# A two-block transformer on one core: h copied and used tile by tile at three heads, and two weight halves moved on ScalarE

## The reference

```python
# first block, two layers: three attention branches on one projection of x, gated, merged, normed
proj = x @ w_in                       # MoBA q k v gate, MLA latents and gate, differential q k v gate
out  = merge(moba(...), mla(...), diff(...)) @ w_out
r    = ALPHA * x + out
x    = layernorm(r + sigmoid(r @ w_pg) * (p @ w_p))

# second block, two layers
def second_block(x, ...):
    for i in range(2):
        h = rmsnorm(x, norm_mix[i])
        x = x + hybrid_mixer(h, ...)      # h @ w_in, short convolutions, a state-space part, a gated norm
        h = rmsnorm(x, norm_ffn[i])
        x = x + (swiglu(h, ...) if i == 0 else moe_swiglu(h, ...))   # 8 experts, top 2
    return rmsnorm(x, norm_final)
```

## Time and profile before

| | us |
|---|---|
| median of three runs | 2121.65 |
| the three runs | 2123.34, 2121.65, 2121.0 |
| the profiled execution | 2121.3 |
| its span in the profile | 2119.5 |
| TensorE busy | 2096.3 |
| VectorE, ScalarE, GpSimd busy | 1416.4, 1295.4, 651.4 |

### The profile page before, as it was taken

The page is one execution under the profiler, slowest core; times in us unless marked ns, Lnnn a source line. Parts: engine busy times, 40 slices in busy tenths (PEclk is TensorE's granted clock), DMA queues, the critical chain, the costliest instruction groups (busy, mean ns, idle before and its releaser), DMA issues.

```text
span 2119.5 us, 33547 instructions
## 1 busy us (share of the span) xinstructions
PE 2096.3 (99%) x13311; PEld 1867.1 (88%) x13315; DVE 1416.4 (67%) x1437; ACT 1295.4 (61%) x1424; POOL 651.4 (31%) x316
## 2 busy tenths in 40 slices
PE   9999999999999999999999999999999999999998
PEld 8979999988999999999998888888888888888887
DVE  1555223346422774223777999999999999999997
ACT  4556545455544534444545777777777777777776
POOL 5717886726787204988101000000000000000000
PEclk9999999999999999999999999999999999999999
DMA  7434564625455425655447999999999999999995
GB/s 245 138 105 153 179 198 156 183 75 163 160 188 177 129 91 175 189 193 178 141 140 252 387 376 336 370 360 376 352 351 370 351 375 351 359 356 375 367 365 200
DMA packets 307633, 529.06 MB, mean 250 GB/s; under 512 B 11842, under 2 KB 152802, under 8 KB 307520
## 3 DMA queue, kind: packets, MB, share of 16 engines
q1 hardware_dynamic: 306496, 525.92, 70.9%
q0 software_dynamic: 736, 1.00, 0.2%
q10 hardware_dynamic: 288, 0.52, 0.1%
HBM read 525.84 MB, written 1.05 MB: 249 GB/s over the span
## 4 chain that ended last, share of the span: by engine, by line
PE 90%; POOL 3%; DVE 3%; ACT 2%; DMA 1%; issue 1%; SPq 0%; DVEq 0%; POOLq 0%
PE bank L720 88%; POOL weights_low L3092 3%; PE bank L1525 1%; DVE qb L2354 1%; DMA ring<-in_w_in_dram 1%; ACT sc L1670 1%; ACT weights_high L1673 0%; DVE sc L2362 0%; DMA ring<-in_w_ple_dram 0%; DVE h L2362 0%; PE bank L929 0%; PE bank L731 0%; DVE nmax L2389 0%; ACT expert_weights_high L1673 0%; ACT xT L1670 0%
## 5 line engine op out<-in xcount | busy, mean ns | idle before, releaser
L2354 DVE TENSOR_TENSOR expert_weights_low<-ring_experts,expert_weights_high 128x2048 fp32r<-128x2048 f32 x336 | 764.7, 2288 | 72.6 <-ACT expert_weights_high L1673 72.5
L1673 ACT ACTIVATE expert_weights_high<-ring_experts 128x2048 fp32r<-128x2048 f32 x336 | 646.4, 1924 | 166.3 <-PE bank L720 162.2
L3092 POOL TENSOR_TENSOR weights_low<-ring,weights_high 128x1024 fp32r<-128x1024 f32 x252 | 617.5, 2474 | 332.0 <-ACT weights_high L1673 218.8
L1673 ACT ACTIVATE weights_high<-ring 128x1024 fp32r<-128x1024 f32 x294 | 303.9, 1056 | 331.7 <-PE bank L720 293.0
L720 PE MATMUL bank<-x_high,weights_high 128*128 128x256 f32 x1024 | 229.8, 281 | 0.5 <-POOL weights_low L3092 0.4
L720 PE MATMUL bank<-x_high,weights_low 128*128 128x256 f32 x1024 | 226.2, 277 | 0.0
L720 PEld LDWEIGHTS bank<-x_high,weights_high 128*128 128x128 f32 x1024 | 183.6, 188 | 2.5 <-POOL weights_low L3092 0.8
L720 PEld LDWEIGHTS bank<-x_high,weights_low 128*128 128x128 f32 x1024 | 183.3, 188 | 0.5 <-issue 0.5
L720 PE MATMUL bank<-expert_weights_high,gathered_high 128*128 128x512 f32 x456 | 180.7, 396 | 0.4 <-DVE gathered_low L2362 0.4
L720 PE MATMUL bank<-expert_weights_high,gathered_low 128*128 128x512 f32 x456 | 177.8, 390 | 0.0
L720 PE MATMUL bank<-expert_weights_high,gathered_high_b 128*128 128x512 f32 x448 | 177.6, 396 | 0.0
(11 more groups left out here) (338 smaller groups left out, 3724.7 us busy)
## 6 DMA issues: line engine op xcount, KB each, us to landing
ring_experts<-in_moe_w_gate_dram SPq DMA_DIRECT2D x112, 1024.0 KB, 6.0
ring_experts<-in_moe_w_up_dram SPq DMA_DIRECT2D x112, 1024.0 KB, 5.8
ring_experts<-in_moe_w_down_dram SPq DMA_DIRECT2D x112, 1024.0 KB, 5.4
ring<-in_w_in_dram SPq DMA_DIRECT2D x62, 1024.0 KB, 5.3
ring<-in_w_merge_dram SPq DMA_DIRECT2D x24, 1024.0 KB, 5.1
ring<-in_w_out_dram SPq DMA_DIRECT2D x14, 1024.0 KB, 5.1
ring<-in_ffn_w_gate_dram SPq DMA_DIRECT2D x11, 1024.0 KB, 5.4
ring<-in_ffn_w_up_dram SPq DMA_DIRECT2D x11, 1024.0 KB, 5.3
```

Source lines behind the costliest of these rows:

```text
L1673: return nc.scalar.activation(dst, src, ACT.Copy, scale=scale)
L2354: return nc.vector.tensor_tensor(dst, x, z, op)
L3092: nc.gpsimd.tensor_tensor(half_of(wlo[:, q_slot, :], t, width), half_of(ring[:, slot, :], t, width), half_of(whi[:, q_slot, :], t, width). ...
```

## The change

It has four parts.

1. At the three heads, the semaphores for "h tile written" and "high part of h made" count single tiles (8) instead of pairs (4), ScalarE copies one tile per instruction, and VectorE's `low_part` waits for the second tile of its pair.
2. TensorE's first projection of each head is `split_project_h`: with `staged=False` (the mixers) both weight halves, high and low, are used on each tile as it comes; with `staged=True` (the feed-forward) the second half's low part follows behind all tiles.
3. In mixer 1 the load of ScalarE's function tables goes ahead of the squares, and the second half of `gv` goes between the second and the third square.
4. In both layers of the first block, half 0 of `after("mc0")` goes ahead of `take_turned(1)`, and half 1 behind `take_y(1)`.

```diff
-        h_part, hh_ready, hl_ready = (signal(n, 4) for n in ("h_tiles_ready", "h_high_ready", "h_low_ready"))
+        h_part, hh_ready, hl_ready = (signal(n, k) for n, k in (
+            ("h_tiles_ready", DT), ("h_high_ready", DT), ("h_low_ready", 4)))
...
+            def split_project_h(b, slot, lo_at, x, count, wait_high, wait_low, staged):
+
+                wh, wl = (w[:, slot, :].rearrange("p (k n) -> p k n", n=S) for w in (whi, wlo))
+                pe.wait_ge(hi_done.h, lo_at + 1)
+                pe.wait_ge(lo_done.h, lo_at + (0 if staged else 1))
+                for kk in range(DT):
+                    wait_high(kk)
+                    for t in range(2):
+                        mm(views(b)[:, t, :], wh[:, kk, t * P:(t + 1) * P], x[0][:, kk, :],
+                           kk == 0 and t == 0, False, share=True)
+                        if t == 0 or not staged:
+                            mm(views(b)[:, t, :], wl[:, kk, t * P:(t + 1) * P], x[0][:, kk, :], False, False, share=True)
+                if staged:
+                    pe.wait_ge(lo_done.h, lo_at + 1)
+                    for kk in range(DT):
+                        mm(views(b)[:, 1, :], wl[:, kk, P:2 * P], x[0][:, kk, :], False, False, share=True)
+                for kk in range(DT):
+                    if kk % 2 == 0:
+                        wait_low(kk // 2)
+                    for t in range(2):
+                        ins = mm(views(b)[:, t, :], wh[:, kk, t * P:(t + 1) * P], x[1][:, kk, :], False,
+                                 kk == DT - 1, share=True)
...
-                        split_project_first(begin(name), *take_split(full2), *wait_h(2 * m))
+                        split_project_h(begin(name), *take_split(full2), *wait_h(2 * m), staged=False)
...
-            split_project_first(0, *take_split(ff_full), *wait_h(1))
+            split_project_h(0, *take_split(ff_full), *wait_h(1), staged=True)
...
                 drain(layer, "dv1", dv[:, :, S:512])
+                after("mc0", (0,))
                 take_turned(1)
+                take_y(1)
+                after("mc0", (1,))
...
-                after("mc0")
-                take_y(1)
                 latent(0)
...
-                for n in range(4):
-                    act.wait_ge(h_part.h, h_part.at(k, n + 1))
-                    copy(hh[:, 2 * n:2 * n + 2, :], h[:, 2 * n:2 * n + 2, :]).then_inc(hh_ready.h, 1)
+                for t in range(DT):
+                    act.wait_ge(h_part.h, h_part.at(k, t + 1))
+                    copy(hh[:, t, :], h[:, t, :]).then_inc(hh_ready.h, 1)
...
                 if m:
+                    act.preload_act_table_set(LOG_EXP)
                     for j in range(4):
                         act.wait_ge(x_up.h, j + 1)
                         square(j).then_inc(sq_ready.h, 1)
-                    act.preload_act_table_set(LOG_EXP)
+                        if j == 1:
+                            split2(SPLITS_M + 1, lambda t: act.wait_ge(ff_down.h, 4 * FD), halves=(1,))
                 b = G2.wait_full(act, m, "ms")
                 inv_std(rs2[:, 0, :], views(b)[:, 0, :], 0, d2a.h, drained2_at("ms")).then_inc(std_ready.h, 1)
-                if m:
-                    split2(SPLITS_M + 1, lambda t: act.wait_ge(ff_down.h, 4 * FD), halves=(1,))
                 high_parts(2 * m)
...
-                dve.wait_ge(hh_ready.h, hh_ready.at(k, n + 1))
+                dve.wait_ge(hh_ready.h, hh_ready.at(k, 2 * n + 2))
```

More of the change, by code:

```diff
@@ L747, in split_project @@
                     ins.then_inc((used if t == 0 else count).h, 1)
+            def split_project_h(b, slot, lo_at, x, count, wait_high, wait_low, staged):
[19 more added lines that the diff above has]
+                                 kk == DT - 1, share=True)
+                        if kk == DT - 1:
+                            ins.then_inc((used if t == 0 else count).h, 1)
             def split_project_low_last(b, slot, lo_at, x, count, halves=(0, 1)):
@@ L1133, in wait_h @@
             def wait_h(k):
-                return (lambda pair: pe.wait_ge(hh_ready.h, hh_ready.at(k, pair + 1)),
+                return (lambda kk: pe.wait_ge(hh_ready.h, hh_ready.at(k, kk + 1)),
                         lambda pair: pe.wait_ge(hl_ready.h, hl_ready.at(k, pair + 1)))
@@ L2602, in mixer @@
                               ALU.mult, ALU.mult)
-                    if t % 2:
-                        ins.then_inc(h_part.h, 1)
+                    ins.then_inc(h_part.h, 1)
                 for n in range(4):
@@ L2799, in norm @@
                     ins = stt(dst[:, t, :], xT[:, t, :], q2[:, w + t:w + t + 1], rs2[:, 0, :], ALU.mult, ALU.mult)
-                    if n == 1 and t % 2:
+                    if n == 1:
                         ins.then_inc(h_part.h, 1)
@@ L3132, in _ @@
                         low2(len(SPLIT2) + g)
-                    pool.wait_ge(h_part.h, h_part.at(1, 4))
+                    pool.wait_ge(h_part.h, h_part.at(1, DT))
                     pool.dma_start(q2[:, :], a["params2"][1, :, :]).then_inc(par2_in.h, 16)
```

## The result

The changed kernel takes 2124.59 us (median of 17 runs, 2120.56 to 2129.54), the kernel before 2121.34 (17 runs beside them). The ratio is 1.0018, with a 95% interval of 1.0012 to 1.0024: 0.18% slower, inside the 0.2% that I had called no change. The forecast was 2123.7. The profiled execution took 2122.13, with a span of 2120.3.

A forecast was written before the change was run, and what follows sets the result against it. TensorE, busy 99% of the span, was taken to bound the kernel. From 2121.3 us, -5.7 for the heads, +5.9 for mc0 and +2.2 for the clock gave 2123.7 us, range 2119 to 2126.5.

The forecast's parts named there:

- the heads: Copies of h tile by tile in mixer 0, feed-forward and mixer 1: -1.25 - 0.35 - 4.1 = -5.7 us together.
- 1:1 at each place: A microsecond won or lost at each changed place reaches the end, since the chain of waits stays on TensorE.
- Part 2, the weight half at mc0: Both attention layers: pT copies wait behind the weights' landing, TensorE idles 4 us; +2.95 us a layer, +5.9 together.
- bracket of 0.84: TensorE's 0.84 us wait for y at mc0, taken as all that moving y's copy ahead can win.
- The clock at that gap: TensorE's 4.0 us idle at mc0 probably lowers its clock: 1.1 us a layer, between 0 and 1.7; +2.2 together.
- Mixer 0 and feed-forward: TensorE starts after one tile of h: -1.25 us in mixer 0, -0.35 us in the feed-forward.
- Mixer 1: GpSimd's subtraction done ahead of h, 48 passes without a wait, ending at 1009.6 instead of 1013.74: -4.1 us.
- Of it 2.1 are VectorE's, and 1.7 are the clock: Split of mixer 1's -4.1 us: VectorE's tiles in 3.26 instead of 5.35, and no lowered clock over 1004 to 1012.
- three slow stretches: Lowered clock in before: at mixer 1's head, costing 1.7 us, and at the narrow step-size matmuls of both mixers.
- Two other stretches ... look the same; I leave them in: Slow clock at the narrow step-size matmuls of both mixers, assumed to remain after the change.
- Slower by a third slow stretch: Rival: clock falls 1.7 us at each new gap and again at mixer 1's head; +5.3, 2126.6 us; chance 0.10.
- Faster, the wait costs nothing: Rival: the wait for az0's weights at mc0 costs nothing, only the heads' -5.7 remains: 2115.6 us; chance 0.12.

The follow-up runs named there:

- e1: Changed kernel with part 4 undone, so the order at mc0 is that of before and the heads stay changed: ratio to before 0.9981, 2117.18 us.
- e2: Kernel before with part 4 alone, weight half 0 ahead of the pT copies and y ahead of half 1: ratio to before 1.0041, 2129.16 us.
- e4: Changed kernel with ScalarE's order at mc0 turned to pT, y, then both weight halves: ratio to before 0.9969, 2115.80 us.
- e3: Changed kernel with 15 extra matmuls on zeros in TensorE's gap ahead of the product with pT, both layers: ratio to before 1.0003, 2121.50 us.
- e7: e1 with mixer 1's table load back behind the squares, the weight half staying between them: ratio to before 0.9978, 2114.69 us.
- e5: Kernel before with part 3 alone, table load and weight half moved in mixer 1, copies of h in pairs: ratio to before 0.9991, 2117.95 us.
- e6: Kernel before with parts 1 and 2 alone, single tiles at the three heads: ratio to before 0.9983, 2116.54 us.
- e8: e4 with mixer 1's table load back behind the squares: ratio to before 0.9959, 2113.60 us.
- e9: e8 with three matmuls on zeros among the 32 narrow step-size matmuls of each mixer: ratio to before 0.9957, 2112.20 us.
- e10: Kernel before with three matmuls on zeros among the narrow step-size matmuls of each mixer, nothing else: ratio to before 1.0001, 2120.32 us.

## Why the prediction was right, and where its terms were off

**The total.** 2123.7 forecast, 2124.59 measured. Taken from the runs, the sum is -4 for the heads (e1, -3.2 by the medians) and +7.4 to +8.7 for mc0 (changed kernel less e1, and e2). The forecast had -5.7 and +8.1. The two parts add up within the measurement, so 1:1 at each place holds. That the total came out within 1 us is in part luck: single terms were off by 0.3 to 1.7 us, in both directions, and largely cancelled.

**Part 2, the weight half at mc0: right in mechanism and nearly in size.** The chain of events came as written: ScalarE idle for 5.53, pT at 99.90 (99.95 forecast), TensorE idle for 3.90 and starting at 101.50 (101.58), no wait for y. The wait itself costs 2.5 us a layer instead of 2.95, because y ahead of the second half gives back 1.5 and not 1.01. The prediction saw in the bracket of 0.84 all that y could win, and counted 1.41 for twelve of the scores; e4 runs all sixteen in 1.6. The size has to be read from the distance of starts.

**The clock at that gap: right in mechanism, low in size.** I took 1.1 between bounds of 0 and 1.7. In the trace each gap has a fall of 1.7 us, of which 1.4 lay on the path in the first layer (e3); if the second is alike, that is 2.7 for the two against 2.2 forecast. Over the timed runs the mean clock is 0.9955 instead of 0.9973, which is 3.8 us, idle time included.

**Mixer 0 and feed-forward.** From VectorE's h to the next group it was 701.26 - 693.54 = 7.72 before and 707.33 - 700.52 = 6.81 now: -0.9 against -1.25. In e7 it was -1.1, at a pass pitch that differs (last section). The feed-forward measured from the weight half: 822.76 - 814.91 = 7.85 before, 827.24 - 819.68 = 7.56 now: -0.3 against -0.35.

**Mixer 1: the step that failed is "Of it 2.1 are VectorE's, and 1.7 are the clock".** The 2.1 are shown (e5 against e6), and over the head the clock did stay at 1.00. But most of the fall's price was not saved. e1 and e5, which have the changed head and not the gap at mc0, have the mean clock of before (0.9974 and 0.9973), and their profiles show a double fall 20 us later. Over all seven kernels with a changed head and no open gap at mc0 (e1, e3 to e8) the falls cost between 1.0 us less and 0.4 more than in before, 0.4 less on average, give or take 0.7; a saving of 1.7 lies outside that. I had named three slow stretches in before and taken them for three separate prices ("Two other stretches ... look the same; I leave them in"). What the runs show is that taking one of them away saved a quarter of its price or so. At full clock the heads gain 4.1 (give or take 0.7), near the forecast's 5.7 without its 1.7. The rows of e1 give less, 0.9 + 0.3 + 3.7 - 1.7 = 3.2; the difference isn't explained. And the head itself gave 3.5 in the changed kernel and not 4.1: TensorE's first pass of h came 6.8 us behind the last pass of the down projection (6.5 before) where I had it no later than before, and the 48 passes took 5.73 and not 5.4.

The corrections together: 1.7 for the clock at mixer 1 (1.3 if 0.4 of it was saved), 0.6 for the rest of mixer 1, 0.5 for the clock at the gaps, 0.4 for mixer 0, and -0.9 for the waits at mc0. The forecast's +2.4 becomes +4.3 to +4.7. Measured is 0.18% of 2121, which is 3.8, with an interval of 2.5 to 5.1. The errors were of both signs, and the largest of them was the clock at mixer 1.

**The rivals.** "Slower by a third slow stretch" is closest to what happened to the clock: the falls of the changed kernel cost 3.8 us more than before's, about the 3.4 of two full falls with none saved, and its runs reach from a mean clock of 0.998 (2120.56 us) to 0.993 (2129.54 us). Three of its 17 runs lie above that rival's 2126.6; the median doesn't. "Faster, the wait costs nothing" is refuted by e2.

**What is still open.** Why the clock falls once at the step-size matmuls of one mixer and twice at those of another, and not at all at mixer 1's in the profile of e6 or at mixer 0's in that of the changed kernel, isn't settled. Each kernel has one profile, and e9 and e10 didn't control it. So it is not shown either that the double fall in e1 and e5 is the one that mixer 1's head lost.

## What to carry to other kernels

Ahead of a wait for a transfer on an in-order engine, put everything that is ready: one weight half that moved ahead of three ready copies cost 3.7 to 4.4 us a layer, and the copy of y moved the other way gained 1.5. Read the price of a wait from the starts of the rows around it, not from its bracket (0.84 stood for 1.5 us). Count a lowered clock as a separate sum over the whole kernel: compare span times mean clock between runs before crediting one place with it, and where a gap stays, try matmuls on zeros in it (2.7 to 3.2 us for two gaps here).

## What the runs showed of the hardware

**A fall of the clock has one size.** In the traces of all twelve kernels every fall up to 2100 us, summed over its windows, came to 1.7 us, or to 3.4 where two ran together, whether an idle gap of 3.9 us or 32 narrow matmuls stood ahead of it. (The first gap of e2 is one of the places with 3.4.) In some kernels these falls make most of the scatter from run to run: the times of e4 have a standard deviation of 3.0 us, its span times clock one of 0.6; for e8 it is 2.1 and 0.35. In others they make less of it: 2.4 and 1.5 for the changed kernel, 1.3 and 1.0 for before in the first set. The Trainium skill, "TensorE: Matmul & The Clock Gate", section "What's actually happening", says that the throttled state is the default and activity releases it; the trace agrees in so far as 3.9 us of idling brought a fall in both layers of the changed kernel, and e3, where zeros filled the gap, had none.

**Passes of one kind run at two paces at the same granted clock.** Sixteen passes of h_low take 2.05 us in mixer 0 of the changed kernel (above, 0.118 each) and 1.98 in e7 (0.1133 each), at a granted clock of 1.00 in both. Such a pace holds over hundreds of passes. In before, mixer 0 ran at the fast one up to its narrow matmuls at 720 and at the slow one behind them, up to 765; in the changed kernel it ran at the slow one up to its narrow matmuls and, but for some 5 us near 745, at the fast one behind them. About a quarter of the stretches of 10 us that hold such passes have the slow one in either kernel, at partly different places; summed over the passes of this shape the difference to the fast one makes 8 to 9 us in both. The 48 passes of a head came out at 5.73 in the changed kernel (701.60 to 707.33) and at 5.54 in e7 (694.41 to 699.95), which explains the 0.2 by which mixer 0's gain differs. I didn't find what selects the pace. The row of e7:

```profile
698.13 1.98 PE L721 MATMUL bank<-h_low,weights_high 128*128 128x256 f32 x16
```
